# Splitting half of three output projections and writing out the last expert pass in a two-block transformer kernel

## The reference, cut to what matters

```
A: x += norm(attention_mixer(norm(x)) )          # ... @ attn_w_out
F0: x += norm(swiglu(norm(x)))
R: x += norm(recurrent_mixer(norm(x)))           # ... @ rg_w_out
F1: x += norm(swiglu(norm(x)))
E: h += dilated_diff_mixer(norm(h))              # ... @ attn_w_out_2
F2: h += swiglu_2(norm(h))
G: h += hgrn2_mixer(norm(h))                     # ... @ hgrn_w_out_2
M: h += moe_swiglu(norm(h))                      # 8 experts, top 2

def moe_swiglu(u, w_router, w_gate, w_up, w_down):
    gates = ...                                  # softmax over the two best experts of a token
    for e in range(N_EXPERTS):
        y = swiglu_2(t, w_gate[e], w_up[e], w_down[e])
        out = out + gates[:, e:e + 1] * y
```

## Time and profile before

| | |
|---|---|
| median of three runs | 2122.27 us |
| the profiled execution, its own time | 2124.49 us |
| its span (first to last instruction) | 2123.0 us |
| PE (TensorE matmul) busy | 2092.1 us, 99% |
| DVE (VectorE) busy | 1386.1 us, 65% |
| ACT (ScalarE) busy | 1179.2 us, 56% |
| POOL (GpSimd) busy | 114.6 us, 5% |

### The profile page before, as it was taken

One profiled execution on the slowest core, in us unless ns is written; L12 is line 12 of the kernel. 1 busy time (PEld: TensorE's weight loads), 2 busy tenths in 40 slices (PEclk: granted clock), 3 DMA queues, 4 the chain that ended last, 5 costly groups with the idle time before them and its releaser, 6 DMA issues.

```text
span 2123.0 us, 26217 instructions
## 1 busy us (share of the span) xinstructions
PE 2092.1 (99%) x10278; PEld 1710.0 (81%) x10278; DVE 1386.1 (65%) x1142; ACT 1179.2 (56%) x1095; POOL 114.6 (5%) x150
## 2 busy tenths in 40 slices
PE   9999999999999999999999999999999999999998
PEld 8757889768888758889876888888888888888777
DVE  1545543454444745442735888888888889888798
ACT  1444441444433644432534778787777777786775
POOL 1000000110000000000002200000000000000250
PEclk9999999999999999999999999999999999999999
DMA  8335555655556226556424999999999999999997
GB/s 280 119 99 200 196 180 159 218 199 187 189 179 207 101 90 218 186 189 217 133 100 175 412 378 391 376 390 372 386 380 375 390 363 393 371 394 376 379 356 271
DMA packets 211781, 561.12 MB, mean 264 GB/s; under 512 B 10558, under 2 KB 67999, under 8 KB 211567
## 3 DMA queue, kind: packets, MB, share of 16 engines
q1 hardware_dynamic: 204224, 530.61, 69.1%
q0 software_dynamic: 5552, 28.84, 3.7%
q10 hardware_dynamic: 1934, 0.67, 0.1%
HBM read 553.27 MB, written 16.25 MB: 268 GB/s over the span
## 4 chain that ended last, share of the span: by engine, by line
PE 93%; DVE 2%; ACT 1%; issue 1%; DMA 1%; POOL 0%; DVEq 0%; ACTq 0%; SPq 0%
PE ps L2046 14%; PE ps L2048 14%; PE ps L2047 14%; PE ps L523 12%; PE ps L618 5%; PE ps L619 5%; PE ps L620 5%; PE ps L582 5%; PE ps L533 4%; PE ps L661 3%; PE ps L659 3%; PE ps L660 3%; PE ps L2099 1%; PE ps L645 1%; DMA ring<-in_moe_w_up 1%
## 5 line engine op out<-in xcount | busy, mean ns | idle before, releaser
L2042 DVE TENSOR_TENSOR ring_r<-ring,ring_r 128x2048 fp32r<-128x2048 f32 x339 | 769.6, 2312 | 113.1 <-ACT ring_r L2037 112.7
L2037 ACT ACTIVATE ring_r<-ring 128x2048 fp32r<-128x2048 f32 x339 | 634.8, 1913 | 94.6 <-DMA ring<-in_moe_w_gate 67.5
L2046 PE MATMUL ps<-ring_r,arena_r 128*128 128x512 f32 x1344 | 531.5, 395 | 3.6 <-DVE ring_r L2042 2.5
L2047 PE MATMUL ps<-ring_r,arena_r 128*128 128x512 f32 x1344 | 525.1, 391 | 0.0
L2048 PE MATMUL ps<-ring_r,arena_r 128*128 128x512 f32 x1344 | 525.1, 391 | 0.0
L329 DVE TENSOR_TENSOR ring_r<-ring,ring_r 128x2048 fp32r<-128x2048 f32 x99 | 226.8, 2291 | 218.8 <-ACT ring_r L320 218.8
L2046 PEld LDWEIGHTS ps<-ring_r,arena_r 128*128 128x128 f32 x1344 | 253.2, 188 | 55.5 <-DVE ring_r L2042 3.3
L2048 PEld LDWEIGHTS ps<-ring_r,arena_r 128*128 128x128 f32 x1344 | 253.2, 188 | 54.1
L2047 PEld LDWEIGHTS ps<-ring_r,arena_r 128*128 128x128 f32 x1344 | 253.3, 188 | 50.8
L320 ACT ACTIVATE ring_r<-ring 128x2048 fp32r<-128x2048 f32 x99 | 189.3, 1916 | 180.2 <-DMA ring<-in_ffn_w_up 78.4
L523 PE MATMUL ps<-arena,ring 128*128 128x128 f32 (+1 forms) x1600 | 258.3, 322 | 1.4 <-ACT arena L373 1.4
(11 more groups left out here) (353 smaller groups left out, 1638.4 us busy)
## 6 DMA issues: line engine op xcount, KB each, us to landing
ring<-in_moe_w_gate SPq DMA_DIRECT2D x115, 1024.0 KB, 6.8
ring<-in_moe_w_up SPq DMA_DIRECT2D x112, 1024.0 KB, 7.1
ring<-in_moe_w_down SPq DMA_DIRECT2D x112, 1024.0 KB, 6.4
ring<-in_ffn_w_gate SPq DMA_DIRECT2D x33, 1024.0 KB, 5.0
ring<-in_ffn_w_up SPq DMA_DIRECT2D x33, 1024.0 KB, 5.1
ring<-in_ffn_w_down SPq DMA_DIRECT2D x33, 1024.0 KB, 5.0
ring<-in_attn_w_in SPq DMA_DIRECT2D x24, 1024.0 KB, 5.7
ring<-in_hgrn_w_in SPq DMA_DIRECT2D x16, 1024.0 KB, 5.5
```

The source lines that it names most:

```text
L2037: nc.scalar.activation(unit_parts(k)[0], ring[:, slot_of(k), 0:2048], ACT.Copy).then_inc(m_hi, 1)
L2042: nc.vector.tensor_tensor(low, ring[:, slot_of(k), 0:2048], high, ALU.subtract).then_inc(m_lo, 1)
L2046: nc.tensor.matmul(out_, x[:, 0, f, :], w[0], start=first, stop=False)
L2047: nc.tensor.matmul(out_, x[:, 1, f, :], w[0], start=False, stop=False)
```

## The change

Three things are done. In stages A, R and G the last two of the four output units (n = 2, 3) become split products, with the activations they multiply split too (`A_split`, `R_split`, `G_split`); stage E's stay plain. In stages F0 and F1 the splits of the second and third first unit are moved ahead in ACT's and DVE's order, and in stage A the second tile's product n = 1 is moved behind all of the first tile's. In stage M the last pass is written out behind a loop of one pass less; it leaves out the splits and the token transposes for a pass that does not come, puts the result straight from PSUM into `M_y`, and the sum of the gathered rows moves from POOL to DVE, at units 8, 12, 16 and 20 of that pass.

```diff
-        def project_out(w, order=(0, 1, 2, 3)):
-            return [(rows_pair(w, r, False), r) for r in order]
+        def project_out(w, order=(0, 1, 2, 3), raw=4):
+            return [(rows_pair(w, r, n >= raw), r) for n, r in enumerate(order)]
...
-        A_out = project_out(a["attn_w_out"][0], (2, 3, 0, 1))
+        A_out = project_out(a["attn_w_out"][0], (2, 3, 0, 1), raw=2)
...
-        R_out = project_out(a["rg_w_out"][0])
+        R_out = project_out(a["rg_w_out"][0], raw=2)
...
-        G_out = project_out(a["hgrn_w_out_2"][0])
+        G_out = project_out(a["hgrn_w_out_2"][0], raw=2)
...
 # ffn_norm_scalar
             norm_sums(act, k, 0)
+            if has_post(k):
+                highs_to(act, first + 1)
             norm_high(act, k, 0)
             highs_to(act, first + 2)
...
 # ffn_norm_vector
             normalise_tokens(dve, k, 0)
+            if has_post(k):
+                lows_to(dve, first + 1)
             norm_low(dve, k, 0)
             lows_to(dve, first + 1)
             if has_post(k):
+                lows_to(dve, first + 2)
                 post_gain(dve, k, 1)
-                lows_to(dve, first + 2)
                 residual(dve, k, 1)
...
 # out_tensor
+            if split_no[u] is not None:
+                wh, wl = (v.rearrange("p (k n) -> p k n", k=2) for v in (slot_hi(u), slot_lo(u)))
+                for kt in range(2):
+                    xh, xl = (v[:, 2 * (n - 2) + kt, t * P:(t + 1) * P] for v in x_split)
+                    for c in range(2):
+                        o, cs = Y[:, t, c * 512:(c + 1) * 512], slice(c * 512, (c + 1) * 512)
+                        nc.tensor.matmul(o, xh, wh[:, kt, cs], start=False, stop=False)
+                        nc.tensor.matmul(o, xl, wh[:, kt, cs], start=False, stop=False)
+                        mm = nc.tensor.matmul(o, xh, wl[:, kt, cs], start=False, stop=(n == 3 and kt == 1))
...
 # A_tensor
-                if m >= 2:
+                if m >= 6:
+                    pe.wait_ge(s_ol, m - 5)
+                elif m >= 2:
                     pe.wait_ge(a_ot, m - 1)
...
             turn(6)
-            out(1, 1)
             values(6)
             turn(7)
             out(2, 0)
             values(7)
             out(3, 0)
-            out_tensor(pe, A_out, 0, OT, 2, 1)
-            out_tensor(pe, A_out, 0, OT, 3, 1)
+            out(1, 1)
+            out_tensor(pe, A_out, 0, OT, 2, 1, A_split)
+            out_tensor(pe, A_out, 0, OT, 3, 1, A_split)
...
 # R_scalar, R_vector (G_scalar, G_vector alike)
+            for n in range(2, 4):
+                act.wait_ge(r_y, n + 1)
+                nc.scalar.activation(R_split[0][:, 2 * n - 4:2 * n - 2, :], R_y[:, 2 * n:2 * n + 2, :], ACT.Copy).then_inc(s_oh, 1)
             highs_to(act, R_out[3][0] + 1)
...
+            for n in range(2, 4):
+                dve.wait_ge(s_oh, 4 + n - 1)
+                nc.vector.tensor_tensor(R_split[1][:, 2 * n - 4:2 * n - 2, :], R_y[:, 2 * n:2 * n + 2, :],
+                                        R_split[0][:, 2 * n - 4:2 * n - 2, :], ALU.subtract).then_inc(s_ol, 1)
             lows_to(dve, R_out[3][0] + 1)
...
 # M_tensor
-            with pe.Fori(0, n * NE) as i:
+            def expert_pass(i, last=False):
...
+            with pe.Fori(0, n * NE - 1) as i:
+                expert_pass(i)
+            expert_pass(n * NE - 1, last=True)
...
 # M_vector
+            def add_choice(c):
+                dve.wait_ge(m_share, 1)
+                dve.wait_ge(m_back, 16 * (2 * TT))
+                x = X[:, c % TT, :]
+                nc.vector.scalar_tensor_tensor(x, M_back[c], M_share[:, c:c + 1], x, ALU.mult, ALU.add).then_inc(m_x2, 1)
...
+                    if last and k in ADD_AT:
+                        if ADD_AT[k] >= TT:
+                            dve.wait_ge(m_x2, ADD_AT[k] - 1)
+                        add_choice(ADD_AT[k])
...
 # M_gpsimd
-            pool.wait_ge(m_back, 16 * (2 * TT))
-            for c in range(2 * TT):
-                step.link(nc.gpsimd.tensor_scalar(M_back[c], M_back[c], M_share[:, c:c + 1], None, ALU.mult))
-                ins = nc.gpsimd.tensor_tensor(X[:, c % TT, :], X[:, c % TT, :], M_back[c], ALU.add)
```

More of the change, by code:

```diff
@@ L973, in out @@
                 if t == 0:
[L974 removed]
+                    pe.wait_ge(*((a_ot, 2 * n + 2) if n < 2 else (s_ol, 2 * n - 2)))
                     pe.wait_ge(a_sc, 16)
@@ L1057, in output @@
                 act.wait_ge(a_pv, 2 * q + 2)
-                f = q + 4 if q < 4 else q - 4
-                nc.scalar.activation(OT[:, f, :], ps[:, 2 + q % 2, 0:SEQ], ACT.Copy).then_inc(a_ot, 1)
+                if q < 4:
+                    nc.scalar.activation(OT[:, q + 4, :], ps[:, 2 + q % 2, 0:SEQ], ACT.Copy).then_inc(a_ot, 1)
+                else:
+                    act.wait_ge(a_sc, 16)
+                    nc.scalar.activation(A_split[0][:, q - 4, :], ps[:, 2 + q % 2, 0:SEQ], ACT.Copy).then_inc(s_oh, 1)
             for j in range(6):
@@ L1195, in build @@
         halves_of = lambda v, n: v[:, 4 * n:4 * n + 4, :]
+        R_split = [page_r(9)[:, 1024 * v:1024 * v + 1024].rearrange("p (f t) -> p f t", t=SEQ) for v in range(2)]
         r_x, r_xc, r_gates, r_sig, r_ix, r_tau, r_exp, r_mult, r_one, r_u, r_h, r_y = (
@@ L1687, in build @@
         G_rs = page(4).rearrange("p (u n) -> p u n", u=4)
+        G_split = [page_r(9)[:, 1024 * v:1024 * v + 1024].rearrange("p (f t) -> p f t", t=SEQ) for v in range(2)]
         pair = lambda v, u: v[:, 2 * u:2 * u + 2, :].rearrange("p f t -> p (f t)")
@@ L1862, in G_scalar @@
             evac(15)
+            for n in range(2, 4):
+                act.wait_ge(g_y, n + 1)
+                nc.scalar.activation(G_split[0][:, 2 * n - 4:2 * n - 2, :], G_o[:, 2 * n:2 * n + 2, :], ACT.Copy).then_inc(s_oh, 1)
+            highs_to(act, G_out[3][0])
         def G_vector(dve, step):
@@ L1960, in G_vector @@
                 nc.vector.tensor_tensor(o, o, pair(G_g, u), ALU.mult).then_inc(g_y, 1)
+            for n in range(2, 4):
+                dve.wait_ge(s_oh, 6 + n - 1)
+                nc.vector.tensor_tensor(G_split[1][:, 2 * n - 4:2 * n - 2, :], G_o[:, 2 * n:2 * n + 2, :],
+                                        G_split[0][:, 2 * n - 4:2 * n - 2, :], ALU.subtract).then_inc(s_ol, 1)
+            lows_to(dve, G_out[3][0])
         LOGIT, OH0, OH1, MASK, GATE, POS, TMP, CUM = (rt[:, n, :].rearrange("p (t e) -> p t e", t=TT) for n in range(8))
@@ L2141, in M_tensor @@
                         turn(i, TURN_AT[k])
-                    if k == TOKENS_AT:
+                    if k == TOKENS_AT and not last:
                         pe.wait_ge(m_x, 16 * i + 16)
@@ L2197, in M_scalar, with expert_pass @@
                 tokens_high(half, GATHER_BANK[2 * half])
-            with act.Fori(0, n * NE) as i:
+            def expert_pass(i, last=False):
                 for k in range(NU):
@@ L2201, in M_scalar @@
                         split_high(act, i, k + AHEAD)
-                    else:
+                    elif not last:
                         split_high(act, i + 1, k + AHEAD - NU)
@@ L2209, in M_scalar @@
                     for half in range(2):
-                        if k == TOKENS_AT + 1 + 2 * half:
+                        if k == TOKENS_AT + 1 + 2 * half and not last:
                             act.wait_ge(m_xt, 2 * i + (half + 1))
@@ L2213, in M_scalar @@
                 act.wait_ge(m_used, NU * i + NU)
-                nc.scalar.activation(M_made.rearrange("p (h n) -> p h n", h=2), ps[:, 5:7, :], ACT.Copy).then_inc(m_y, 1)
-            act.wait_ge(m_y, n * NE + 1)
-            nc.scalar.activation(M_y[:, 0, 0:512], M_made[:, 0:512], ACT.Copy).then_inc(m_yh, 1)
+                if not last:
+                    nc.scalar.activation(M_made.rearrange("p (h n) -> p h n", h=2), ps[:, 5:7, :], ACT.Copy).then_inc(m_y, 1)
+                    return
+                for h in range(2):
+                    nc.scalar.activation(M_y[:, 0, 512 * h:512 * h + 512], ps[:, 5 + h, :], ACT.Copy).then_inc(m_yh, 1)
+            with act.Fori(0, n * NE - 1) as i:
+                expert_pass(i)
+            expert_pass(n * NE - 1, last=True)
         def M_vector(dve, step):
```

97 lines of the change are left out of this document (57 added, 40 removed).

## The result

The changed kernel takes 2109.68 us, the median of five runs (2106.73 to 2111.98), where the kernel before takes 2122.13 beside it: a ratio of 0.994 (0.9925 to 0.9954). A second measurement of the same kernel gave 2105.74 (2104.77 to 2109.06) against 2123.06, a ratio of 0.9919 (0.9905 to 0.9932). The profiled execution of before stood on the other side of its median, 2.4 us above 2122.13, so the two profiles show 5 us more between them than the first pair of medians does.

The account below looks back on a forecast made before the run. TensorE, 93% of the span, bounds the kernel, with waits ending on DVE. Terms 3.9 (A) + 3.0 (R) + 2.7 (G) + 5.4 + 0.9 (last pass) + 0.8 (tail) = 16.7 us; 2122.27 - 16.7 = 2105.6 us, range 2101.5 to 2112.

Parts of the forecast that it names:

- The price, 0.67 us for each unit and tile: Output products of A, R, G: split costs 2.76 us against 3.43 plain, saving 0.67 each, 8.1 us over 12.
- the five places of the walk: Stage A to tile 1 of F0: five PE waits (values, out(3, 0), first low half, up 1, second tile), 5.5 us.
- Stage R: To F1: 2.7 us from split products plus a 1.8 us shorter norm chain, less new waits; 3.0 us gained.
- a wait of about 0.3 us: Stage R: a new PE wait because the second unit's split, its load landing after 5.1 us, precedes the norm's halves.
- 5.4 + 0.9: Stage M's last pass: 5.4 us from sums moved to DVE, 0.9 us from eight token transposes left out.
- the first wait, 2.1 us: Last pass: PE waits for the gated product behind a split with late weights during the gathers; 2.1 us stay.
- The second wait: Last pass, second turn: PE waits 1.1 us where it waited 1.9, with sums on DVE.
- Late weights hold the last pass: Rival, last pass: late weights, not POOL, cause the waits, so the 5.4 us stay; 2111 us, 12%.
- Splits too late for the output products: Rival, A, R, G: PE waits at n = 2, gain some 4 us smaller; 2110 us, 10%.
- Sums on DVE hold it up: Rival, last pass: late gathers or 2.6 us sums lose up to the 5 us again; 2111 us, 5%.
- Code of the written-out pass: Rival, last pass: PE waits for newly loaded instructions, up to 25 us; 2131 us, slower, 3%.
- The change does little: Rival, output products: split cadence no better than plain, only stage M's 7 us gained; 2115 us, 2%.

Follow-up runs that it names:

- e1: The kernel before with only the changed kernel's stages A, R and G, stage M as before: 2113.16 us, ratio 0.9954.
- e9: The changed kernel with stage E's last two output units split as well: 2105.03 us, ratio 0.9917.
- e3: The changed kernel with the gathered rows scaled and added on POOL again, last pass still written out: 2113.12 us, ratio 0.9955.
- e12: The changed kernel with later sums, gain ahead of third unit's split, fillers before the first expert pass, fewer tail fillers, and stage E's split: 2102.28 us, ratio 0.9904.
- e5: The changed kernel with the second unit's split behind the norm's halves again, ahead of F1 only: 2108.12 us, ratio 0.9928.
- e2: The kernel before with only the changed kernel's stage M (written-out last pass, sums on DVE, shorter tail): 2115.05 us, ratio 0.9963.
- e4: The changed kernel measured again, unchanged: 2105.74 us (2104.77 to 2109.06), ratio 0.9919.
- e7: The changed kernel with the four DVE sums at units 16, 20, 24, 28 of the last pass: 2105.23 us, ratio 0.9915.
- e11: The changed kernel with later sums, gain ahead of third unit's split, fillers before the first expert pass, two tail fillers for six: 2103.89 us, ratio 0.9915.
- e10: The changed kernel with eight small filler matmuls on PE ahead of the first expert pass: 2105.52 us, ratio 0.9918.

## Why the prediction was right, and where it was off

The forecast of 2105.6 lay 4 us under the first median and in the range; the second median, 2105.74, is on it. The sum was 16.7 us and the profiled spans differ by 17.7, but the medians by 12.45 and 17.3. That the second median falls on the forecast is in part luck: the first lies 4 us off, and in the spans a last pass that gained 1.65 us more than its terms made up for 0.65 too little in R and 0.3 in the tail.

One sentence of the prediction does not hold: that nothing in the sum depends on the profiled execution of before standing 2.2 us above the median. The 5.4 us of the last pass have 1.6 for the stretch at the low clock, and in e1, whose stage M is that of before, that stretch is missing. How often the kernel before has it was not measured; where it has not, the gain is 1.6 us less.

*The split output products (A, R, G).* The price, 0.67 us for each unit and tile, held. In G 2.56 of 2.7 us arrived, PE never waited at n = 2, and e9 shows the same price in a stage that the change had left out. Stage A came out at 4.07 for 3.9, its waits at the five places of the walk with 4.9 us for 5.5.

*Stage R* is the term that was off: 2.35 for 3.0. The step that failed is "its load ... lands 5.1 us later", with "a wait of about 0.3 us". At a landing of 5.1 the wait is 0.27 us, to the tenth as predicted (e3, e12). But this load takes 5.1 to 7.4 us from one execution to the next, and I had taken its time from a single row in another stage. In the old order the load stood behind the norm's halves: at a landing of 7.3 us PE has no wait at that matmul (e5), and the other two profiles with the old order, before and e2, both have a landing of 5.0, so they can't show it. The new order puts the norm's high half behind the load on ACT, and every tenth of a microsecond of landing then moves PE. That accounts for part of the spread. e5 shows that it can't be had back by putting the split behind again, since the fourth unit pays.

*The last pass.* 7.95 us for 5.4 + 0.9. The term that was mis-sized is "Left are 2.1 + 1.1 + 0.5 refill = 3.7 us": 2.0 are left in the first profile (9.06 - 7.95 + 0.87), 2.6 on average over the eight. The direction and the cause were right (e3: 5.7 us come back with the sums on POOL, and DVE's rows with them), the size too small by 1.65. The prediction kept the first wait, 2.1 us, on the ground that late weights cause it, "That stays": the first profile has no wait there, e2 0.6, e4 1.8, e7 0.55. It varies with the moment at which the weights arrive: ACT starts the split ahead of the gated product when its load has landed, at 1996.89 in the first profile and at 2001.27 in e4, 2.9 us later in its pass. The second wait, predicted at 1.1, was 0.96 to 0.99 us in six profiles, and e7 confirms that there it is the first sum on DVE. In the first profile it was 1.83, for a late weight load, and in e4 0.4. The sum of both, predicted at 3.2, was 1.6 to 2.4 us in the eight profiles.

*The tail.* 0.52 for 0.8. The fillers set it, as the walk said, but PE was through with them 1.56 us behind the last unit (2095.99 to 2097.55) and not at 1.05; e11 got the missing half microsecond by taking four of them out.

*The rivals.* Late weights hold the last pass: not the 5.4 us, by the first profile and e3; but late weights make the 1.83 us of the first profile and the waits at the first turn. Splits too late for the output products: in no profile does PE wait at n = 2 (L592); at n = 3 of stage A it waits the 0.97 us of the walk. Sums on DVE hold it up: true for 1.1 us, not for 5. Code of the written-out pass: by the page queue q8 has 56 packets where before had 52, and the first profile has PE in the last pass at rest for nothing but the 1.83 us. The change does little: no.

*What the prediction left out* is the variation from run to run. Two levels of the clock behind the first expert matmul (1.4 us) and the landing ahead of F1 (2.3 us) together give 3.7 us, and e10 shows that a long wait can bring a stretch at the low clock on top (F0 to F1 are 289.76 us there, 1.3 more than in e4 for a landing that is 0.3 later); the five runs of the first measurement span 5.2. That these are the causes in the runs that were not profiled is argued, not shown. Why the load takes 5.1 us in one execution and 7.4 in another stays open: the DMA engines had moved nothing for some 11 us before it, and the next load is issued 3.4 us behind it at either landing.

## What to carry to other kernels

Work that is moved ahead of a norm on a queue makes everything behind it wait for its data as well: price it with the slowest landing that the traces show, not with one row. A cheaper product is also a shorter cover; when two are made cheaper, look at once at what they hid, as the moved n = 1 does here. And element-wise work beside a busy VectorE can be best given to VectorE itself, if a trace shows its rows stretched beside GpSimd's: four sums cost DVE 5.1 us here, and its 45 splits in the last pass take 2.285 us each in place of 2.481 (e3), 8.8 us less.

## What the runs showed of the hardware that was not expected

- A 1 MB load issued onto idle DMA engines landed after 5.1 to 7.4 us in twelve executions, though it was issued 262.8 to 262.9 us behind tile 1 of F0 in every one.
- The granted clock fell to 0.50 (1.2 GHz) behind a rest of 1.14 to 1.25 us at the start of stage M in six executions, and stayed at 1.00 behind one of 1.14 to 1.22 in five. It fell behind a rest of 2.53 us (e10) and stayed at 1.00 behind 2.23 (e4) and 2.37 us (e5). Fillers on PE in place of the rest kept it up in three of three profiles, where without them it stayed up in five of eleven.
- POOL's row on a 128x1 tile took 2.14 and 2.41 us beside a DVE split and 0.30 alone, and the split was not slowed (2.28 us). With 128x1024 rows on POOL both were: 4.78 us on POOL, 4.13 for the split.
